# Hybrid block, one core: the entry of the feed-forward part rebuilt (tiles one step behind the mix, residual and operand sums on DVE, the second pair's two plain products ahead of the combined ones)

## The reference

```python
mix = jnp.concatenate([y_mla, y_pool], axis=-1) @ w_o[l]
x = x + gt1 * mix

h = rmsnorm(x, g_ffn[l]) * (1.0 + sc2) + sh2
ff = (jax.nn.silu(h @ w_gate[l]) * (h @ w_up[l])) @ w_down[l]
x = x + gt2 * ff
return rmsnorm(x, g_final)
```

## Time and profile before

| what | us |
|---|---|
| median of 3 runs | 1113.09 (1112.45 to 1115.05) |
| the profiled execution | 1111.35 |
| its span | 1109.5 |
| PE busy / DVE busy / ACT busy / POOL busy | 1001.4 / 689.3 / 449.4 / 383.4 |

### The profile page before, as it was taken

One profiled execution on the slowest core, in us unless ns is written; L12 is line 12 of the kernel. 1 busy time (PEld: TensorE's weight loads), 2 busy tenths in 40 slices (PEclk: granted clock), 3 DMA queues, 4 the chain that ended last, 5 costly groups with the idle time before them and its releaser, 6 DMA issues.

```text
span 1109.5 us, 12566 instructions
## 1 busy us (share of the span) xinstructions
PE 1001.4 (90%) x4605; PEld 817.8 (74%) x4605; DVE 689.3 (62%) x973; ACT 449.4 (41%) x765; POOL 383.4 (35%) x272
## 2 busy tenths in 40 slices
PE   5699699999999935589999999999998999699996
...
PEclk9799799999999977789999999999999999899999
...
GB/s 335 309 10 105 58 1 6 71 1 77 1 266 216 109 111 57 55 107 190 209 133 124 181 216 98 132 209 173 103 170 207 306 208 378 201 198 209 208 58 152
DMA packets 119545, 165.20 MB, mean 149 GB/s; under 512 B 8310, under 2 KB 61370, under 8 KB 119484
## 3 DMA queue, kind: packets, MB, share of 16 engines
...
HBM read 124.26 MB, written 40.11 MB: 148 GB/s over the span
## 4 chain that ended last, share of the span: by engine, by line
PE 64%; DVE 14%; ACT 6%; POOL 5%; DMA 5%; issue 4%; SPq 2%; POOLq 0%; DVEq 0%; ACTq 0%
PE PS L1980 35%; PE PS L2018 14%; PE PS L1689 8%; DMA ADA<-in_w_ada 2%; PE PS L1863 2%; PE PS L1748 2%; DVE ACC L1231 2%; DVE GT L1231 2%; DMA REraw<-t_scratch 1%; ACT HBf L1017 1%; ACT HTf L1017 1%; DVE W L1243 1%; DVE HT L1243 1%; PE PS L1875 1%; POOL ropeQ L692 1%
## 5 line engine op out<-in xcount | busy, mean ns | idle before, releaser
L2018 PE MATMUL PS<-RE 128*128 128x512 f32 x924 | 210.6, 390 | 0.0
L2018 PEld LDWEIGHTS PS<-RE 128*128 128x128 f32 x924 | 173.7, 188 | 36.9 <-issue 1.0
L1243 DVE TENSOR_TENSOR RE<-REraw,RE 128x1024 fp32r<-128x1024 f32 x77 | 109.3, 1448 | 84.0 <-ACT RE L1091 82.6
L1980 PE MATMUL PS<-HB,WS 128*128 128x512 f32 x528 | 125.7, 394 | 22.8 <-issue 22.8
L1980 PE MATMUL PS<-HT,W 128*128 128x512 f32 x528 | 124.5, 394 | 19.5 <-DVE W L1243 19.5
L1980 PEld LDWEIGHTS PS<-HB,WS 128*128 128x128 f32 x528 | 100.6, 191 | 44.7 <-issue 23.6
L1091 ACT ACTIVATE RE<-REraw 128x1024 fp32r<-128x1024 f32 x77 | 81.0, 1062 | 128.6 <-DMA REraw<-in_w_down 64.3
L1980 PE MATMUL PS<-HT,WS 128*128 128x512 f32 x528 | 127.9, 399 | 5.6 <-ACT PV L1074 2.8
L1980 PEld LDWEIGHTS PS<-HT,W 128*128 128x128 f32 x528 | 100.3, 191 | 41.1 <-DVE W L1243 20.2
L1980 PEld LDWEIGHTS PS<-HT,WS 128*128 128x128 f32 x528 | 102.1, 194 | 28.1 <-issue 6.4
L1554 DVE TENSOR_TENSOR SG<-PS,PV 128x512 f32<-128x512 f32 x22 | 15.2, 691 | 121.0 <-PE PS L1980 115.7
...
## 6 DMA issues: line engine op xcount, KB each, us to landing
...
REraw<-h_scratch SPq DMA_DIRECT2D x77, 256.0 KB, 4.5
h_scratch<-SG SPq DMA_DIRECT2D x55, 256.0 KB, 2.4
...
t_scratch<-TW SPq DMA_DIRECT2D x44, 256.0 KB, 2.9
REraw<-t_scratch SPq DMA_DIRECT2D x44, 256.0 KB, 5.2
REraw<-in_w_down SPq DMA_DIRECT2D x33, 256.0 KB, 5.3
...
```

Source lines behind the costliest of these rows:

```text
L1243: dve.tensor_tensor(out_, full, hi.bitcast(F32), ALU.subtract).then_inc(ready, 1)
L1980: ins = pe.matmul(PS[:, bank, :], l, r, start=fresh and z == 0, stop=z == len(terms) - 1, skip_group_check=not fresh)
L2018: ins = pe.matmul(PS[:, D_BASE[p] + j, :], RE[e][:, a, 0, tok(j)], RE[e][:, b, 1, :], start=p in (1, 2, 7) and i == 0 and x_ == 0, stop=i ...
```

## The change

What it does, part by part:

1. **Residual on DVE.** The addition of MIX to X for mixes 8 to 15 moves from POOL to DVE, right behind `gated`.
2. **Tiles one step behind the mix.** `turn_x(0)` stands behind mix 9, tiles 1 and 2 behind mix 11, tiles 3 to 6 behind mixes 12 to 15; before, tiles 0 to 5 stood behind mixes 10 to 15. `col_sum(7)` goes from behind mix 11 to behind mix 10, and the MOD and G2 columns are made at tile 2 instead of 3. Only `turn_x(7)` is left among the stages.
3. **First weights.** The HI half of pair 0's plain weights is made by POOL from W12first into W12 (it was a copy by ACT of a second load of the same weights, which is gone), the LO half for product 1 on DVE at tile 6.
4. **Operand sums on DVE.** `t_sums` and the two 128x2048 operations of POOL are replaced by seven DVE operations on 256 or 512 tokens (`t3_sum`, `t2_sum`, `t1_sum`); two of pair 0's four weight sums move to DVE (`w_sum_first`), into a new buffer WSfirst.
5. **Order of stages.** (0,1) (0,2) (1,1) (1,2), then pair 0's 6, 5, 7, 3, 4, then pair 1's; from pair 2 on as before. Pair 1's plain weights have a buffer of their own, W12next, which lies over WO1 and over the slots of products 7 and 3, so pair 0's operands of 7 and 3 are made after stage (1, 2).
6. **SP.** W12next is loaded behind mix 15; `load_tw(0)` waits for pair 0's last operand, and `tw_away(0)` goes from the middle of pair 0 to its end.
7. **Last pair and down projection.** ACT's `d_hi(0, 1, 2)` and `d_hi(3, 4, 5)` stand behind the copies of product 6 and of product 5, ahead of which they stood; `col_sum(8)`, `col_sum(9)` go from ahead of block (6, 3) to ahead of block (5, 3), and DVE's copy of GT2 from step 34 to step 51.

The diff, cut to its core:

```diff
-    STAGES = [(p, m) for p in (1, 2, 6, 5, 7, 3, 4) for m in range(2)]
+    P_ORDER = (1, 2, 6, 5, 7, 3, 4)
+    STAGES = [(0, 1), (0, 2), (1, 1), (1, 2)] + [(n, p) for n in range(2) for p in P_ORDER[2:]]
+    STAGES += [(n, p) for n in range(2, NC) for p in P_ORDER]
+    STAGES = [(n, p, m) for n, p in STAGES for m in range(2)]
...
@@ SP
-        sp.wait_ge(S["x_out0"], 64)
-        load_w12(0)
...
+        x_away(6, S["x_out2"])
+        sp.wait_ge(S["mix_done"], 2 * NT)
+        for m, src in enumerate((gate_d, up_d)):
+            sp.dma_start(W12nextraw[:, LO, m], src[:, :, P:2 * P]).then_inc(S["w12next_in"], 16)
+        x_away(7, S["x_out2"])
...
             if n == 0:
-                sp.wait_ge(S["x_new"], 2 * NT)
+                sp.wait_ge(S["w_ready"], w_ready_at(0, 3))
...
-            tw_away(n)
+            if n >= 1:
+                tw_away(n)
...
             h_away(3, n, ST[:, 1, :], "a12_out")
+            if n == 0:
+                tw_away(0)
@@ POOL
+        for t in range(3):
+            h2_hi(t)
+        w12_first_hi()
+        h2_hi(3)
+        w_sums_first()
+        w_sums(1)
+        tw_sums(0)
@@ ACT
+            for b in {2: (0,), 3: (1,), 4: (2, 3), 5: (4,), 6: (5,), 7: (6,)}.get(t, ()):
+                modulate2(b)
...
+            copy_out(n, 6, 0)
+            copy_out(n, 6, 1)
             if last:
                 d_hi(0, 1, 2)
-            copy_out(n, 6, 0)
-            copy_out(n, 6, 1)
@@ DVE
+        def x_add(t):
...
+            dve.tensor_tensor(X[:, t, half(1)], X[:, t, half(1)], MIX[t % 2][:], ALU.add).then_inc(S["x_new"], 1)
...
         for t in range(NT):
-            gated(NT + t, 1)
-            if t == 3:
+            if t == 2:
...
+            gated(NT + t, 1)
+            x_add(t)
             if t < 2:
                 accumulate(14 + t)
             if 3 <= t < 7:
                 h2_lo(t - 3)
+            if t == 6:
+                w12_first_lo(1)
             if t == 7:
-                t_lo(4)
-                w_lo(0, (1, 2))
-        xn2(NT - 1)
-        t_lo(5)
+                t3_sum(0)
+            xn2(t)
+        w12_first_lo(2)
+        t2_sum(0)
+        w12_next_lo(1)
+        w12_next_lo(2)
+        t3_sum(1)
+        t2_sum(1)
+        t2_lo(0)
+        t2_lo(1)
+        w_sum_first(3)
+        w_lo(0, 6)
+        t1_sum()
+        w_lo(0, 5)
+        w_sum_first(7)
...
-            if z == last_step(6) + 2:
+            if z == last_step(5) + 8:
                 gate(2)
                 gate(3)
@@ PE
-            if m >= NT + 2:
-                if m == NT + 3:
-                    col_sum(7)
-                turn_x(m - NT - 2)
+            if m == NT + 2:
+                col_sum(7)
+            for t in {NT + 1: (0,), NT + 3: (1, 2), NT + 4: (3,), NT + 5: (4,), NT + 6: (5,), NT + 7: (6,)}.get(m, ()):
+                turn_x(t)
...
-            if (p, a0) == (6, 3):
+            if (p, a0) == (5, 3):
                 pe.wait_ge(S["d_add"], B["d_add"] + 4)
                 col_sum(8)
                 col_sum(9)
```

More of the change, by code:

```diff
@@ L344, in h_of, with count, w_ready_at, w_hi_at @@
         return HT[:, part, k + (HK if p in (2, 3) else 0), half(1 if p in (3, 5) else 0)]
-    LOS = {5: 1, 7: 2, 1: 3, 6: 4, 3: 5, 2: 6, 4: 7}
-    N_LO = 7
+    LO_ORDER = [(1, 2, 6, 5, 4, 7, 3), (5, 7, 6, 3, 4)] + [(5, 7, 1, 6, 3, 2, 4)] * (NC - 2)
+    HI_ORDER = [(6, 5, 4, 7, 3), (5, 6, 7, 3, 4)] + [(1, 5, 6, 7, 3, 4)] * (NC - 2)
+    def count(orders, n, p):
+        return sum(len(o_) for o_ in orders[:n]) + orders[n].index(p) + 1
+    def w_ready_at(n, p):
+        return count(LO_ORDER, n, p)
+    def w_hi_at(n, p):
+        return count(HI_ORDER, n, 1 if p == 2 else p)
+    SUM_AT = [{5: 1, 6: 2, 3: 3, 7: 4}] + [{5: 4 * n + 1, 6: 4 * n + 2, 7: 4 * n + 3, 3: 4 * n + 4} for n in range(1, NC)]
     D_ORDER = (1, 2, 6, 5, 7, 3, 4)
@@ L1091, in d_hi @@
                 act.activation(RE[e][:, HI], REraw[e][:, LO], ACT.Copy).then_inc(S["d_hi"], 1)
-        for n in range(NC):
+        copy_out(0, 1, 0)
+        copy_out(0, 1, 1)
+        w_hi(0, 6)
+        t2_hi(1)
+        w_hi(0, 5, 4)
+        part_hi(HT[:, HI, 0:HK, half(1)], HTf[:, 0:HK, half(1)], 3)
+        w_hi(0, 7, 3)
+        copy_out(0, 6, 0)
+        act.wait_ge(S["w_sum"], 4)
+        act.wait_ge(S["w_ready"], 2)
+        part_hi(HB[:, HI, 1], HBf[:, LO, 1], 2)
+        copy_out(0, 6, 1)
```

355 lines of the change are left out of this document (196 added, 159 removed).

## The result

| what | before | after |
|---|---|---|
| median, us | 1112.77 (4 runs, 1110.40 to 1115.05) | 1073.89 (4 runs, 1072.65 to 1077.92) |
| the profiled execution, its span | 1111.35, 1109.5 | 1072.65, 1070.6 |

The ratio is 0.9653, with a 95% interval of 0.9623 to 0.9683: 38.9 us faster by the medians. The forecast was 1062, so 12 us of the expected gain are missing.

What follows compares the result with a forecast made beforehand. PE's work bounds the kernel, plus its waits and lower-clock stretches. The entry gains 57 - 20.2 = 36.8 us and the late parts 13.8, together 50.6 from 1111.35: 1060.7, forecast as 1062 us, 8-in-10 range 1052 to 1077.

Steps and rivals of the forecast that it cites:

- the shared port: Tile 5 to (0,6): POOL's copies and sums cost 6.9 us if DVE waits out each, else nothing; only in the range.
- (1,6): Into pair 1: this stage waits 1.7 us for ACT's copies for W22 and of (1,1), with no clock price.
- The terms of the entry's loss: New entry: PE waits of 15.6 us plus 4.6 of lower clock, together 20.2 us.
- tile 0: Before mix 10: PE waits 8.1 us for XN(0), there at 363.0, plus 2.3 for the clock.
- (1,3): Pair 1: PE waits 4.5 us for ACT's copies behind W12, late in SP's queue, plus 2.3 of clock.
- 57: Entry before the change, `col_sum(6)` to the end of pair 1: 47.7 us idle plus 9.2 lower clock, together 57 us lost.
- Tiles 1 to 6 and the operand chain: Entry: PE held only 0.4 us, at tile 6; stages begin near 405; operand waits 0.5 at (0,2), 0.4 at (0,3).
- Rival 2: DVE bounds the entry: waits at (0,6), (0,5) or (0,7), 7 to 12 us worse, 1069 to 1074; chance 0.23.
- Rival 1: SP's queue into pair 1 isn't late, so no wait at (1,3): 6.8 us better, 1055; chance 0.17.
- Rival 3: Down projection's wait only moves, to block (5, 3) or a late ring step: 9.3 less gain, 1071; chance 0.11.
- Rival 4: Waits at tile 0 and later tiles hold PE at its lower clock: 63 us more, 1125; chance 0.02.
- The late parts: Last pair's wait and clock loss go, 4.5 us, and the down projection's, 9.3: both together 13.8.

Runs made afterwards that it cites:

- e: Changed kernel with POOL's four weight sums of pair 1 replaced by zero fills and its four TW sums of pair 0 cut to 8 columns: 1065.32 us.
- f: Changed kernel with W12 of pair 2 loaded on SP as soon as POOL's last sum of pair 1 is done: 1070.22 us.
- d: Changed kernel with pair 1's two plain products behind pair 0's products 6 and 5, ACT's copies for 7 and 3 following: 1085.75 us.
- a: Changed kernel with the second gate's two broadcasts ahead of block (6, 3) again and DVE's copy behind step 34: 1086.54 us.
- b: Changed kernel with ACT's copies of ring steps 0 to 5 ahead of the copies of products 6 and 5 again, last pair: 1076.64 us.
- j: Changed kernel with the residual additions of mixes 8 to 15 back on POOL: 1074.21 us, ratio 0.9661.
- c: Changed kernel with tile 0's transposes behind mix 10 again, 1 behind mix 11, and so on, tiles 5 and 6 behind mix 15: 1069.50 us.

## Why the prediction was right, and where it was off

Right in sign and within the range; the mechanism held, and one choice in the sum failed.

- **Failed: "I put none into the sum" for the shared port.** The bound of 6.9 us was worked out for the stretch from tile 5 to (0,6), and of that only the delays of tiles 5 and 7 came. The larger part came where the forecast had not looked for it, at the end of pair 0: POOL's sums for pair 1 and for TW beside DVE's sums of h, 7.7 us. The prediction itself had named both POOL's TW sums "beside DVE" and the row of 3.36 against 1.22, but let the stretched time count only for SP's chain, and priced (1,6) by ACT's two copies alone: 1.7 forecast, 9.81 measured, 1.78 once the contention is gone (e).
- **The terms of the entry's loss** (20.2 forecast): tile 0, 8.1 forecast, 6.40 measured, with 1.7 in the clock (transposes 1.97 for 1.09, and the six matmuls behind them); 0.4 forecast at tile 6 and 0.44 measured at tile 5; (0,2), 0.5 forecast, 2.26 at tile 7 ahead of it and 1.7 of clock (7.31 for 5.60); (0,3), 0.4 and none; (1,6), 1.7 forecast, 9.81 and 1.5; (1,3), 4.5 and 2.3 forecast, 3.58 and 2.6 measured. That is 30.0. Another 1.8 is no part of the change: PE reached the end of `col_sum(6)` at 363.07 - 6.40 = 356.7 instead of 354.9, mostly because the clock fell behind the wait ahead of mix 8 (granted 0.90 from 340 to 357 us, 1.00 in the trace before). Together 31.8, and 57 - 31.8 is 25.2, against the 25.3 measured.
- **Where the terms agree by luck.** Tile 0's chain was right to the tenth: XN(0) was there at 363.0. The wait is shorter than forecast only because PE came 1.8 late, and 6.40 + 1.8 is 8.2, for the 8.1 forecast. The 0.44 is no late LO half of W12, which cost nothing at tile 6: at tile 5 an addition and a subtraction of DVE took 1.16 and 2.06 us beside POOL's copies, instead of 0.69 and 1.22. At (1,3) PE and SP's chain were both late by about 9 us: ACT's copy of W12 came at P + 29.0 instead of P + 20.1, behind DVE's `h_last` and not behind POOL's sums of TW, and PE came at P + 27.9 instead of P + 18.0. Their difference stayed near the forecast.
- **Tiles 1 to 6 and the operand chain** were right: stages from 405.27 (forecast about 405), and no wait at (0,6), (0,5), (0,7), (0,3) or (0,4). The sign "no PE wait over 2 us from there to (1, 6)" failed at tile 7 (2.26). Rival 2 was right that the rest comes from contention and gave the right size, 1069 to 1074, but for waits at (0,6), (0,5) or (0,7), where there was none.
- **Rival 1** (SP's queue not late) is refuted by the wait of 3.58 and by f, where the earlier load takes it away. **Rival 3** is refuted: 1.40 us is all that came in place of 8.36. **Rival 4** too: within eight transposes and six matmuls of the wait at tile 0, PE's rows were back at their shorter durations.
- **The late parts**, 13.8 forecast and 13.6 in the trace. Taken back alone they cost 13.5 (9.3 forecast) and 3.6 (4.5 forecast); the sum of the two is more than both together gave, because each wait is partly hidden behind the other's: alone, the gate's wait is 3.2 longer, and with the last pair's wait back the 1.40 is gone.
- **Part by part**, the change's gain is in the order of the stages (d), the gate's place (a) and the last pair's order (b). The move of the residual to DVE gave nothing that the ratios can tell (j), and the tiles' earlier turns lost 4 us (c), which the forecast had accepted with its 8.1 + 2.3 at tile 0 without asking what leaving the turns in place would give. Parts 3, 4 and 6 (first weights, operand sums on DVE, SP's order) were not taken back alone, so how the rest of the entry's gain divides among them is not shown.
